# A diffusion-transformer layer in one kernel: the first modulation and the k product of the first five token tiles in four quarters of the channels instead of two halves

## The reference, cut to what matters

```python
mod_x = silu(c) @ w_ada + b_ada              # 6 * 1024 values for the latent tokens
mod_c = silu(c_ctx) @ w_ada + b_ada          # the same for the context tokens
sh1, sc1, g1, sh2, sc2, g2 = split(mod_x, 6)
h_x = rms_norm(x, norm1_gain) * (1 + sc1) + sh1
h_c = rms_norm(ctx, norm1_gain) * (1 + csc1) + csh1
u, q, k, v, g, ga, gb = split(h_x @ w_in)    # k and v also from h_c
# Fourier mixing of u, two-way retention of q, k, v, then
y = (sigmoid(ga) * y_four + sigmoid(gb) * y_ret) @ w_out
x = x + g1 * y
x = x + g2 * (relu(modulate(rms_norm(x), sh2, sc2) @ w1) ** 2 @ w2);  out = rms_norm(x)
```

## Time and profile before

| | |
|---|---|
| time, median of 3 runs | 1274.85 us (1274.56 to 1275.66) |
| profiled execution, its own time | 1275.49 us |
| its span | 1273.7 us |
| TensorE busy | 1252.3 us, 98% of the span, 6248 matmul records |
| VectorE, ScalarE, GpSimd busy | 888.5, 606.4, 163.3 us |
| chain that ended last | TensorE 86%, DMA 6%, VectorE 4% |
| granted TensorE clock | 0.999 of full speed |

### The profile page before, as it was taken

The page is one execution under the profiler, slowest core; times in us unless marked ns, Lnnn a source line. Parts: engine busy times, 40 slices in busy tenths (PEclk is TensorE's granted clock), DMA queues, the critical chain, the costliest instruction groups (busy, mean ns, idle before and its releaser), DMA issues.

```text
span 1273.7 us, 16993 instructions
## 1 busy us (share of the span) xinstructions
PE 1252.3 (98%) x6248; PEld 1032.7 (81%) x6248; DVE 888.5 (70%) x1400; ACT 606.4 (48%) x1031; POOL 163.3 (13%) x112
## 2 busy tenths in 40 slices
PE   7999999999999999999999999999999999999997
PEld 4788788888987878787788888888888888888886
DVE  5672587668659887787688665565556669768866
ACT  7661211244436343433677555455445433554444
POOL 0125420142250000125510000000000000000000
PEclk9999999999999999999999999999999999999999
DMA  9414220103285455596732544444448985477534
GB/s 366 183 35 156 77 98 2 34 19 100 84 289 207 153 170 196 176 379 232 264 133 85 200 163 148 146 162 147 137 156 286 316 292 185 159 237 255 192 105 160
DMA packets 95226, 219.18 MB, mean 172 GB/s; under 512 B 11532, under 2 KB 11932, under 8 KB 95144
## 3 DMA queue, kind: packets, MB, share of 16 engines
q1 hardware_dynamic: 82752, 182.70, 41.7%
q10 hardware_dynamic: 8728, 22.29, 4.8%
q0 software_dynamic: 3664, 13.11, 3.1%
HBM read 166.66 MB, written 51.39 MB: 171 GB/s over the span
## 4 chain that ended last, share of the span: by engine, by line
PE 86%; DMA 6%; DVE 4%; ACT 1%; issue 1%; POOL 1%; SPq 1%; ACTq 0%; DVEq 0%
PE ps L2992 14%; PE ps L2994 14%; PE ps L2993 14%; PE ps L3617 8%; PE ps L3625 8%; PE ps L3620 8%; PE ps L3455 3%; PE ps L3457 3%; PE ps L3460 3%; PE ps L3643 3%; PE ps L3033 2%; DMA raw<-in_w_stream 2%; PE ps L3075 1%; PE ps L3242 1%; DMA ada_a<-in_ada_stream 1%
## 5 line engine op out<-in xcount | busy, mean ns | idle before, releaser
L2992 PE MATMUL ps<-t_hi,s_hi 128*128 128x512 f32 x392 | 153.3, 391 | 0.0
L2993 PE MATMUL ps<-t_lo,s_hi 128*128 128x512 f32 x392 | 153.0, 390 | 0.0
L2994 PE MATMUL ps<-t_hi,s_lo 128*128 128x512 f32 x392 | 153.0, 390 | 0.0
L1792 ACT ACTIVATE s_hi<-s_raw 128x512 fp32r<-128x512 f32 x112 | 70.6, 630 | 115.3 <-DMA b<-in_w_stream 59.4
L1053 POOL TENSOR_TENSOR ring_lo<-raw,ring_hi 128x1024 fp32r<-128x1024 f32 (+2 forms) x37 | 86.2, 2343 | 194.8 <-ACT ring_hi L1179 191.3
L2871 DVE TENSOR_TENSOR s_lo<-s_raw,s_hi 128x512 fp32r<-128x512 f32 x112 | 77.3, 690 | 44.2 <-ACT s_hi L1792 43.6
L2992 PE MATMUL ps<-ring_hi,hT_hi 128*128 128x512 f32 x224 | 91.2, 407 | 0.0
L2994 PE MATMUL ps<-ring_hi,hT_lo 128*128 128x512 f32 x224 | 87.5, 391 | 0.0
L2993 PE MATMUL ps<-ring_lo,hT_hi 128*128 128x512 f32 x224 | 87.4, 390 | 0.0
L2992 PEld LDWEIGHTS ps<-t_hi,s_hi 128*128 128x128 f32 x392 | 73.6, 188 | 16.0 <-DVE t_lo L2875 0.3
L2994 PEld LDWEIGHTS ps<-t_hi,s_lo 128*128 128x128 f32 x392 | 73.6, 188 | 15.8
(11 more groups left out here) (511 smaller groups left out, 3210.0 us busy)
## 6 DMA issues: line engine op xcount, KB each, us to landing
s_raw<-ff_scr SPq DMA_DIRECT2D x112, 256.0 KB, 2.9
raw<-in_w_stream SPq DMA_DIRECT2D x34, 512.0 KB, 4.3
ff_scr<-ffs SPq DMA_DIRECT2D x16, 1024.0 KB, 4.8
t_raw<-in_w_stream SPq DMA_DIRECT2D x64, 256.0 KB, 3.3
w_B_raw<-in_w_stream SPq DMA_DIRECT2D x48, 256.0 KB, 2.7
ff_scr<-ffa SPq DMA_DIRECT2D x16, 768.0 KB, 4.6
b<-in_w_stream SPq DMA_DIRECT2D x48, 256.0 KB, 4.4
ada_next<-in_ada_columns POOLq DMA_DIRECT2D x13, 512.0 KB, 4.3
```

Of the source, the lines that this page charges most:

```text
L1792: A(s_slot[n][0][:], s_slot[n][2][:], ACT.Copy).then_inc(down_hi, 1)
L2992: M(dst, lhsT=l_hi, rhs=r_hi, start=first, stop=False, skip_group_check=goes_on)
L2993: M(dst, lhsT=l_hi, rhs=r_lo, start=False, stop=False, skip_group_check=goes_on)
L2994: return M(dst, lhsT=l_lo, rhs=r_hi, start=False, stop=last, skip_group_check=goes_on)
```

## The change

Tiles 0 to 4 are done in quarters p of the channels (two blocks of 128) instead of halves. `FIRST` is the order of the (tile, quarter) parts: tiles 0 to 3 for p = 0, 1, 2, then tile 4 for these, then all five for p = 3. The layout of `ada_stream` on the host changes, so that four pieces of 512 KB hold one quarter; a matmul of `ada_part` now has 128 columns in place of 256, and there are eight of them for a piece. SyncE's order becomes: tile 0, tile 1, four pieces, k0, tiles 2 and 3, four pieces, k1, four pieces, tile 4, k2, four pieces, k3, tile 5. All modulation of these tiles is VectorE's. The exponentials and columns of the decay go behind the first parts. GpSimd takes the remainder of k1 from VectorE. In the gates the rows 8 and 11 get a new place behind `four_part` in rounds 2 and 3, and rows 9 to 15 come earlier by up to two places. Unchanged lines stand in the diff where they show the new order; removed ones are shown only in part.

```diff
-SIDE = [("x", _s, 0) for _s in range(EARLY)] + [("x", _s, 1) for _s in range(EARLY)]
+FIRST = [(_n, _p) for _p in range(3) for _n in range(EARLY - 1)] + [(EARLY - 1, _p) for _p in range(3)]
+FIRST += [(_n, 3) for _n in range(EARLY)]
+FIDX = {c: i for i, c in enumerate(FIRST)}
+LATER = 3 * EARLY
+SIDE = [("x", _n, _p) for _n, _p in FIRST]
...
+        def part_buf(i):
+            return h_f[:, i % 4 * 256:(i % 4 + 1) * 256].rearrange("p (c t) -> p c t", c=2)
         def x_tile(s):
             return ctx_in[:, s, :] if s < 2 else x_a[:, s - 2, :] if s < 6 else x_b[:, s - 6, :]
+        def ada_piece(p, k):
+            i = 4 * (p % 2) + k
+            if p < 2:
+                return ada_a[:, i, :], ht_landed[i]
+            return ada_b[0][:, i, :] if i < 4 else ada_b[i // 2 - 1][:, i % 2, :], ada_b_in[i]
+        def load_part(eng, p):
+            for k in range(4):
+                place_, landed = ada_piece(p, k)
+                eng.dma_start(place_, ins["ada_stream"][p, k]).then_inc(landed, 16)
...
+            load_part(sp, 0)
             for i, (kind, n) in enumerate(STREAM):
+                if i == 1:
                     load_x(sp, 2)
                     load_x(sp, 3)
+                    load_part(sp, 1)
+                if i == 2:
+                    load_part(sp, 2)
+                    load_x(sp, 4)
+                if i == 3:
+                    load_part(sp, 3)
                 if i in (2, 3):
                     sp.dma_start(raw_of(i), ins["w_stream"][WIDX[(kind, n)]]).then_inc(k_in[i - 2], 16)
                     continue
...
-                    sp.wait_ge(ada_done, 2)
+                    sp.wait_ge(ada_done, 4)
                     for s in (6, 7, 8, 9):
...
-            lo(INDEX[("k", 0)])
-            pool.wait_ge(split, INDEX[("k", 2)])
-            for i in range(INDEX[("k", 2)], INDEX[("q", 2)]):
+            for i in range(INDEX[("k", 0)], INDEX[("q", 2)]):
                 lo(i)
...
+            def first_hi(n, p):
                 hi_ap, _, _ = h_tile(TILES[n])
+                side_out(act, ("x", n, p))
+                A(hi_ap[:, 2 * p:2 * p + 2, :], part_buf(FIDX[(n, p)]), ACT.Copy).then_inc(hhi_done, 1)
...
             A(lw[:, 3, :], lw[:, 2, :], ACT.Ln).then_inc(decay_exp, 1)
             square(0)
             square(1)
             root_of(0)
             norm(0)
             root_of(1)
             norm(1)
+            hi_to(("k", 0))
+            first_hi(0, 0)
+            first_hi(1, 0)
             square(2)
             root_of(2)
             norm(2)
             square(3)
             root_of(3)
+            first_hi(2, 0)
             norm(3)
+            hi_to(("k", 1))
+            first_hi(3, 0)
+            first_hi(0, 1)
+            act.wait_ge(decay_log, 3)
+            A(dec[:], dec[:], ACT.Exp).then_inc(decay_exp, 1)
+            first_hi(1, 1)
+            act.wait_ge(decay_log, 4)
+            A(dmask[:], dmask[:], ACT.Exp).then_inc(decay_exp, 1)
+            first_hi(2, 1)
+            first_hi(3, 1)
+            hi_to(("k", 2))
+            first_hi(0, 2)
             square(4)
             root_of(4)
+            first_hi(1, 2)
             norm(4)
+            first_hi(2, 2)
+            first_hi(3, 2)
             hi_to(("k", 3))
+            for p in range(3):
+                first_hi(4, p)
+            first_hi(0, 3)
+            first_hi(1, 3)
             square(5)
             root_of(5)
+            first_hi(2, 3)
             norm(5)
+            first_hi(3, 3)
+            first_hi(4, 3)
             copy_kc(0)
...
+            def first_modulate(n, p):
+                i = FIDX[(n, p)]
                 r = 1 if n < 2 else 0
+                dve.wait_ge(side_done, i + 1)
+                if i > 3:
+                    dve.wait_ge(h_ready, i - 3)
+                for q in range(2):
+                    c = 2 * p + q
+                    ins_ = V.tensor_scalar(part_buf(i)[:, q, :], ps[:, side_bank(("x", n, p)), q * P:(q + 1) * P],
+                                           a1[:, c, r:r + 1], mod[:, c, r:r + 1], ALU.mult, ALU.add)
+                ins_.then_inc(side_free[i % 2], 1)
+            def first_lo(n, p):
+                i = FIDX[(n, p)]
+                hi_ap, lo_ap, _ = h_tile(TILES[n])
+                cs = slice(2 * p, 2 * p + 2)
+                dve.wait_ge(hhi_done, i + 1)
+                V.tensor_tensor(lo_ap[:, cs, :], part_buf(i), hi_ap[:, cs, :].bitcast(F32), ALU.subtract
+                                ).then_inc(h_ready, 1)
...
+            def mod_columns(p):
+                cs = slice(2 * p, 2 * p + 2)
+                dve.wait_ge(ada_done, p + 1)
+                if p:
+                    dve.wait_ge(modT_done, p)
+                V.tensor_copy(mod_rows[:, 0:P], ps[:, 4, 0:P]).then_inc(rows_done, 1)
+                dve.wait_ge(modT_done, p + 1)
+                def both(x):
+                    return x[:, cs][:, :, None].to_broadcast([P, 2, 2])
+                rows = ps[:, 4, 256:256 + P].rearrange("p (q z) -> p q z", q=4)[:, :, 0:2]
+                do(V.tensor_tensor(mod[:, cs, :], rows[:, 0:2], both(bmod1[:, 0:KT]), ALU.add))
+                do.chain(V.tensor_tensor(rows[:, 2:4], rows[:, 2:4], both(gain1[:]), ALU.mult))
+                V.tensor_tensor(a1[:, cs, :], rows[:, 2:4], both(gained_b[:]), ALU.add).then_inc(mod_ready, 1)
+                dve.wait_ge(mod_ready, 3 + p)
             mod_columns(0)
...
+            first_modulate(0, 0)
+            first_modulate(1, 0)
+            first_lo(0, 0)
+            first_lo(1, 0)
+            decay_powers(range(0, 3))
             tokens_mean(2)
             tokens_rstd(2)
+            decay_powers(range(3, HEADS))
+            first_modulate(2, 0)
             tokens_mean(3)
             tokens_rstd(3)
+            first_lo(2, 0)
+            first_modulate(3, 0)
+            mod_columns(1)
+            first_lo(3, 0)
+            first_modulate(0, 1)
+            first_modulate(1, 1)
+            first_lo(0, 1)
+            first_modulate(2, 1)
+            first_lo(1, 1)
+            first_modulate(3, 1)
+            first_lo(2, 1)
+            first_lo(3, 1)
+            decay_columns()
+            mod_columns(2)
+            first_modulate(0, 2)
+            first_modulate(1, 2)
+            first_lo(0, 2)
             tokens_mean(4)
             tokens_rstd(4)
+            first_modulate(2, 2)
+            first_lo(1, 2)
+            first_modulate(3, 2)
+            first_lo(2, 2)
+            first_lo(3, 2)
+            decay_mask()
+            mod_columns(3)
+            first_modulate(4, 0)
+            first_modulate(4, 1)
+            first_lo(4, 0)
+            first_modulate(4, 2)
+            first_lo(4, 1)
+            first_lo(4, 2)
+            first_modulate(0, 3)
+            first_modulate(1, 3)
+            first_lo(0, 3)
+            first_modulate(2, 3)
+            first_lo(1, 3)
             tokens_mean(5)
             tokens_rstd(5)
+            first_modulate(3, 3)
+            first_lo(2, 3)
+            first_modulate(4, 3)
+            first_lo(3, 3)
+            first_lo(4, 3)
             dve.wait_ge(params_in, 16 * 5)
...
                 g_los(j + 1, LATER_UNITS[2:])
-                add_row(3 + 2 * j)
+                add_row((5, 7, 10, 13)[j - 1])
                 g_add("12", j)
                 heads_part(j)
                 four_part(j)
+                if j in (2, 3):
+                    add_row((8, 11)[j - 2])
                 g_sums(j + 2)
                 g_los(j + 2, LATER_UNITS[:2])
-                add_row(4 + 2 * j)
+                add_row((6, 9, 12, 14)[j - 1])
                 both_parts(j)
                 g_add("11", j + 1)
             g_add("22", 5)
             g_los(6, LATER_UNITS[2:])
-            add_row(13)
             g_add("12", 5)
+            add_row(15)
             g_sums(7)
             g_los(7, LATER_UNITS[:2])
-            add_row(14)
             heads_part(5)
             four_part(5)
             both_parts(5)
             g_add("11", 6)
-            add_row(15)
...
+            def k_part(n, p, passes=("hh", "lh", "hl"), middle=None):
                 i = MIDX[("k", TILES[n])]
                 dst = ps[:, main_bank(i), :]
                 l_hi, l_lo, _ = h_tile(TILES[n])
+                r_hi, r_lo = slot(("k", p))
+                for kind in passes:
+                    if kind == "lh":
+                        pe.wait_ge(h_ready, FIDX[(n, p)] + 1)
+                    else:
+                        pe.wait_ge(hhi_done, FIDX[(n, p)] + 1)
+                    pe.wait_ge(*((split if kind == "hl" else hi_done), p + 1))
+                    for e in range(2):
+                        kt = 2 * p + e
+                        mm = M(dst, lhsT=(l_lo if kind == "lh" else l_hi)[:, kt, :],
+                               rhs=(r_lo if kind == "hl" else r_hi)[:, e * 512:(e + 1) * 512],
+                               start=kind == "hh" and kt == 0, stop=kt == KT - 1 and kind == passes[-1])
```

(71 more changed lines are left out.)

232 lines of the change are left out of this document (42 added, 190 removed).

## The result

The changed kernel takes 1289.5 us (median of 4 runs, 1289.0 to 1290.4); the kernel before took 1274.7 beside it. The ratio is 1.0123, with an interval of 1.011 to 1.0136: 14.8 to 15.7 us slower, where I had forecast 9.0 more and 1289.5 as the upper end. The sign was right, the size too small.

A forecast was written before the change was run, and what follows sets the result against it. TensorE's own work and waits were taken as the bound. Start -5.4, work +4.4, waits +8.3 and gate rows +1.6 gave 8.9, rounded 9.0: 1283.8 us as a median, range 1273.5 to 1289.5.

The forecast's parts named there:

- The start, 5.4 forecast: First k product on TensorE: starts at 17.3 us instead of 22.66, a gain of 5.4 us.
- Modulation records, 33 ns forecast: Early modulation on TensorE: 192 records of 128 columns at 33 ns each, 6.3 us, 2.6 more than before.
- The rival of 58 ns: Early modulation: records keep 58 ns each, 4.8 us more, total about 1288 us; chance 0.09.
- Seven cost 1.1, bounds 0 and 2: TensorE's early products: seven more blocks of modulation pieces between them cost 1.1 us for changes between narrow and full weights.
- Transposes, 0.7 forecast: TensorE before tile 6: four more transposes, one more row transpose and 20 groups for 10 cost 0.7 us.
- Work as a whole, 4.4 forecast: TensorE from first k product to tile 6's transposes: 4.4 us more work, bounds 2.6 and 10.1.
- Waits that come in: 8.3 us: TensorE from first k product to tile 6's transposes: new waits on other engines, 8.3 us in all.
- The three quarter turns: First product of a quarter directly behind its transposes: TensorE waits 1.2 us at each of three, 3.6 in all.
- The clock, put at nothing in the sum: TensorE's clock might fall in the thin stretch from 14 to 17 us and cost more; no size given.
- Behind it TensorE runs full as before, so all of it reaches the end: After tile 6's transposes, forecast at 66.8 us: TensorE stays full, so the whole 7.4 us delay reaches the end.
- The rows in the gates, 1.6 more forecast: Gates: moved modulation rows add 3.2 us of waits for sig_b, less 1.6 for uv; net 1.6, bounds 0 and 5.
- The lead is kept: Early tiles: TensorE doesn't wait (under 1 us), tile 6's transposes come at 58.5 us, so faster; chance 0.15.

The follow-up runs named there:

- decay first: The changed kernel with all decay powers, exponentials, columns and mask back at the start; 1291.1 us, ratio 1.0118.
- clock held: The changed kernel with idle matmuls (8, 12 and 18) put into three of TensorE's waits; 1290.5 us, ratio 1.0128.
- Blocks split: The kernel before, still in halves, with groups of four transposes cut in two and two modulation blocks cut into five; 1276.6 us, ratio 1.001.
- GpSimd later: The changed kernel with GpSimd's subtraction for the first two weight chunks held until VectorE has written its first remainders; 1289.3 us, ratio 1.0105.
- norm first: The changed kernel with tile 6's square, root and norm ahead of ScalarE's context k copies and second modulation of tile 5; 1290.7 us, ratio 1.0123.
- other order: The changed kernel with the next quarter's first transposes ahead of tile 3's product and the remainder pass last; 1283.2 us, ratio 1.0074.
- all four edits: The changed kernel with GpSimd's first remainder later, tile 6's norm earlier, idle matmuls (8, 4, 4) in gaps and TensorE's order changed; 1285.1 us, ratio 1.0084.
- the run with the chunk first: The kernel before with SyncE loading the first output chunk ahead of modulation row 16; 1276.9 us, ratio 1.0005.
- front only: The changed kernel with the modulation rows of the gates back in their old places, so the four quarters alone; 1290.5 us, ratio 1.0116.

## Why the prediction was right in sign and too small

- **The start, 5.4 forecast, 6.06 measured.** Right as walked (0.6 of it was a start 0.6 earlier of all work on c). Other executions with the same start have the first product up to 1.45 us later, so this term is known to about 1 us only. That it counts in full is wrong: the run with the decay first starts 4.0 us later and ends the retention 1.2 later.
- **Modulation records, 33 ns forecast.** 30 in a block of 48 (1.45 us from 38.10 to 39.55), 36 in blocks of 16, 34 over all with the clock held. The rival of 58 ns is out, and so is the Trainium skill's second price in "TensorE: Matmul & The Clock Gate", section "Wait — 56ns, not 53.3ns?": no record took 62. Right.
- **"Seven cost 1.1, bounds 0 and 2".** Near enough. Blocks split gives some 0.18 on the products for each further modulation block, 1.3 for seven; by the rows of clock held it was 0.8. The other growth of the products, 2 us with the clock held, comes mostly with the waits.
- **Transposes, 0.7 forecast, 1.8 measured.** Four rows of transposes ahead of waits take 0.24 each more than otherwise, 1.0 in all. The 0.8 that is left is the 0.7 forecast.
- **Work as a whole, 4.4 forecast.** With the clock held it grew by 7.9. Less 1.8 in rows ahead of waits it is 6.1, and less 0.12 behind each of eight waits about 5.1. The term was right to within 1 us, and "the lead is nearly eaten by work alone" stands.
- **"Waits that come in: 8.3 us": the step that failed first.** 10.85 were noted, and some 13 with the rows ahead of them. The three quarter turns, forecast 1.2 each, took 1.05, 1.11 and 1.06. The remainder passes, 0.9, 0.9 and 0.7 forecast, took 0.46, 0.69 and 0.47. Tiles 2 and 3 took 0.85 and 1.06, near the 2.2 forecast, although 0.75 of the second was VectorE held by GpSimd. Unforeseen were the 1.68 for `hc_lo`, for the same reason, and the 2.42 for tile 6: 4.1 us. The prediction gave a remainder 0.41 us everywhere and looked at GpSimd's chunk only as done in time, not as something that stops VectorE; the runs show 2.72 for two remainders beside it.
- **The clock, put at nothing in the sum.** The prediction named its fall as what would make the forecast wrong, for "the thin stretch from 14 to 17 us", and gave it no price. In this execution it fell between 19 and 20, behind the wait of 1.68, and between 74 and 75, behind that of 2.42: 1.3 to 1.9 and 1.7 us. In GpSimd later, norm first and other order it did fall at 16 to 17 us.
- **"Behind it TensorE runs full as before, so all of it reaches the end": false.** ScalarE's list for tile 6 was hidden in the kernel before because it was done 1.45 us before TensorE came. With the quarters ScalarE's last copy comes at the end of the early products, and the list behind it is bare. Norm first tried one other order of ScalarE's list, and the wait came out at other places; whether another order removes it was not tried.
- **The rows in the gates, 1.6 more forecast, nothing measured.** The two waits came, 1.63 and 1.39, together 3.0 for my 3.2. But 1.1 of waits for sig_b was there before, which I had not taken off: 1.9 more, less the 1.6 for uv, as forecast. 0.3 was left in the pairs, and both kernels' gates span 154.5.
- **The rivals.** "The lead is kept" set 58.5 as the mark without waits. By all four edits it would be between 59 and 60, so its mark was about right; its condition, waits under 1 us, was not met in any version.

Sum by measured terms at tile 6: -6.06 for the start, 3.3 for products, 2.8 for modulation and 1.8 for transposes with the clock held, 1.9 for the clock, 10.85 of waits, 14.6. Behind it 1.7 for the clock again: 16.3. By the end of the gates it is 15.9, behind them -2.3 in this execution, and 14.8 between the medians. That the median came no further than the upper end of the range is luck: the loss at the end of retention was 16.3 where 7.4 was forecast, the 1.6 forecast for the gates did not come, and nothing in the prediction foresaw the 2.3 behind them.

## What to carry to other kernels

Finer stages buy an earlier start with smaller pieces, each of which passes through the whole chain of engines again. Compare the added work with the lead first: here the two were about equal (5 to 6 us each), so every wait behind them was a loss. Then look at each engine in the chain for what else it does at that time. The two waits that were not foreseen came from work that had been hidden: GpSimd's subtraction beside VectorE's remainders, and ScalarE's list for the next tile. Count cuts by changes of kind and not by rows of a timeline, and take the time that a row ahead of a wait runs out as part of the wait. Price a fall of the clock behind a long wait (1.3 to 1.9 us here). Filling or moving a single wait often brings out the next: GpSimd's block went from the remainders to the decay powers, and once more appeared in the gates when a chunk came early. Take the order of issue first, which alone gave back 3.7 us by the marks and 6 by the medians.

## What of the hardware I had not expected

- A remainder on VectorE (two inputs in SBUF, 256 columns, 0.41 us) stood still while GpSimd's subtraction of 1024 columns ran: 2.72 us for two, 0.95 with GpSimd moved. Three decay powers went from 0.88 to 2.87 when GpSimd's subtraction ran beside them, and GpSimd's own from 2.36 to 3.29. In the gates of the run with the chunk first three remainders of 512 columns took 4.10 for 1.89.
- Idle stretches of 1.68 and 2.42 us were each followed by some 3 us at the clock level 0.50, although TensorE was busy all through these 3 us. A wait of 2.15 us in the run with the chunk first was followed by the same, in the midst of the gates, and so was one of 1.9 in front only. But the same wait of 1.68 in front only was followed by no fall (1.00 in every window from 16 to 34 us), nor were those of 1.05 to 1.11 at the turns, those of 1.63 and 1.39 in the gates of the changed kernel, and the 1.60 of the earlier trace rows before. In norm first a wait of 1.10 at 14.55 was followed by 0.50 from 16 to 22.5, twice as long. So the length of one wait alone doesn't tell it; what else it takes stays open.
- Between transposes and float32r products a change is nearly free: the pair of products behind takes 0.09 us more, and two transposes take less than half of four (0.14 for 0.36). A change to and from the 32-column modulation records costs about 0.3 us in all.
